# WKV7 recurrence of a two-block kernel: scores and turns on four quarters of the array, two banks for crossing products, products with v apart, state by scalar products

## The reference

```python
def wkv7_scan(s0, r, w, kk, a, k, v):
    def step(s, inp):
        r_t, w_t, kk_t, a_t, k_t, v_t = inp
        s_kk = jnp.einsum('bhvk,bhk->bhv', s, kk_t)
        s = (s * w_t[:, :, None, :] - s_kk[..., None] * (kk_t * a_t)[:, :, None, :]
             + v_t[..., None] * k_t[:, :, None, :])
        return s, jnp.einsum('bhvk,bhk->bhv', s, r_t)
    xs = tuple(jnp.moveaxis(t, 1, 0) for t in (r, w, kk, a, k, v))
    s_final, ys = lax.scan(step, s0, xs)
    return jnp.moveaxis(ys, 0, 1), s_final
```

## Time and profile before

| | |
|---|---|
| median of 3 runs | 3311.26 us (3309.19 to 3319.1) |
| the profiled execution | 3302.93 us, span 3301.3 us |
| PE busy over the span | 2858.2 us (87%) |
| DVE, ACT, POOL busy | 1932.0, 1372.7, 536.4 us |
| mean granted clock of PE | 0.942 |

### The profile page before, as it was taken

How to read it: one execution, slowest core, us unless ns; L and a number is a source line. 1 busy time by engine, 2 the same in 40 slices (tenths; PEclk the granted TensorE clock), 3 DMA queues, 4 the chain that set the end, 5 groups by cost and what they waited for, 6 DMA issues and landing times. The chain is left out here.

```text
span 3301.3 us, 70036 instructions
## 1 busy us (share of the span) xinstructions
PE 2858.2 (87%) x30245; PEld 2351.2 (71%) x30245; DVE 1932.0 (59%) x3065; ACT 1372.7 (42%) x2028; POOL 536.4 (16%) x489
## 2 busy tenths in 40 slices
PE   7998799989989569999735999999965987769999
PEld 2564678788778448887515999999963754548877
DVE  5431455666565345765663888888875146456652
ACT  2002445444444322212213777777753345333331
POOL 3001445454344110000001000000010025100000
PEclk9999899999999789999966999999987999889999
DMA  4643000000000128664306999999951210122322
GB/s 193 220 153 104 6 20 20 20 20 20 20 3 4 65 87 309 268 252 172 112 15 260 365 371 363 372 371 362 371 207 61 99 53 18 51 78 90 102 101 78
DMA packets 74015, 483.10 MB, mean 146 GB/s; under 512 B 11123, under 2 KB 13043, under 8 KB 32288
## 3 DMA queue, kind: packets, MB, share of 16 engines
q1 hardware_dynamic: 59360, 418.48, 34.0%
q0 software_dynamic: 12096, 52.43, 4.3%
q10 hardware_dynamic: 2304, 8.39, 0.6%
HBM read 457.73 MB, written 34.13 MB: 149 GB/s over the span
## 5 line engine op out<-in xcount | busy, mean ns | idle before, releaser
L2156 DVE TENSOR_TENSOR sb_moe_w_lo<-w_ring,sb_moe_w_hi 128x1408 fp32r<-128x1408 f32 (+1 forms) x132 | 255.2, 1934 | 67.7 <-ACT sb_moe_w_hi L2110 67.5
L2056 PE MATMUL ps<-sb_moe_w_hi,sb_x_feat_lo 128*128 128x352 f32 x832 | 274.3, 330 | 11.5 <-DVE sb_moe_w_lo L2156 11.5
L2058 PE MATMUL ps<-sb_moe_w_hi,sb_x_feat_hi 128*128 128x352 f32 x832 | 268.4, 323 | 0.0
L2057 PE MATMUL ps<-sb_moe_w_lo,sb_x_feat_hi 128*128 128x352 f32 x832 | 267.8, 322 | 0.0
L2110 ACT ACTIVATE sb_moe_w_hi<-w_ring 128x2816 fp32r<-128x2816 f32 x80 | 204.1, 2553 | 0.1
L2056 PEld LDWEIGHTS ps<-sb_moe_w_hi,sb_x_feat_lo 128*128 128x128 f32 x832 | 157.0, 189 | 17.3 <-issue 17.0
L2056 PE MATMUL ps<-sb_moe_w_hi,sb_hid_feat_lo 128*128 128x256 f32 x572 | 163.3, 285 | 3.9 <-DVE sb_hid_feat_lo L2182 3.9
L2058 PE MATMUL ps<-sb_moe_w_hi,sb_hid_feat_hi 128*128 128x256 f32 x572 | 161.9, 283 | 0.0
L2057 PE MATMUL ps<-sb_moe_w_lo,sb_hid_feat_hi 128*128 128x256 f32 x572 | 161.9, 283 | 0.0
L1321 DVE STREAM_TRANSPOSE sb_tb<-sb_tb 128x128 f32<-128x128 f32 x384 | 106.0, 298 | 93.6 <-ACT sb_tb L1230 91.5
L231 PE MATMUL ps<-sb_ffn_features,sb_hi_ffn 128*128 128x512 f32 x352 | 140.2, 398 | 22.1 <-DVE sb_lo_ffn L219 22.1
(11 more groups left out here) (511 smaller groups left out, 7924.3 us busy)
## 6 DMA issues: line engine op xcount, KB each, us to landing
w_ring<-w_moe_up SPq DMA_DIRECT2D x67, 1408.0 KB, 8.3
sb_hm<-w_ada SPq DMA_DIRECT2D x48, 1024.0 KB, 6.9
w_ring<-w_ffn SPq DMA_DIRECT2D x22, 1024.0 KB, 4.8
w_ring<-w_up SPq DMA_DIRECT2D x22, 1024.0 KB, 4.9
sb_t_again<-w_moe_up SPq DMA_DIRECT2D x13, 1408.0 KB, 8.5
sb_hm<-w_moe_up SPq DMA_DIRECT2D x13, 1408.0 KB, 8.3
sb_b_again<-w_moe_up SPq DMA_DIRECT2D x13, 1408.0 KB, 7.9
w_ring<-w_moe_down SPq DMA_DIRECT2D x13, 1408.0 KB, 7.6
```

The source lines that it names most:

```text
L2056: pe.matmul(out, x_lo, w_hi, start=first, stop=False)
L2057: pe.matmul(out, x_hi, w_lo, start=False, stop=False)
L2058: return pe.matmul(out, x_hi, w_hi, start=False, stop=end)
L2156: return V.tensor_tensor(WL[:, s, w], raw[raw_at(c, i)[0]][:, w], WH[:, s, w].bitcast(F32), ALU.subtract)
```

## The change

`score` and `trans` become one item. Products with FB and turns of FA and FK stay on the head's own quarter, in bank `i`; products with FK and turns of FB and v go from the head's rows to the other head's columns (`both_ways`), into one of two crossing banks, 4 + i mod 2. The order alternates: two own, two crossing. The masks are then applied in two operations (`LKE` on the own bank, `LKO` on the crossing one), and ACT copies in two (`trO`, then `trE`).

`akv` is split. `akA` stands ahead of the quad's scores, four in a row, each in its own bank. `akO` holds all that doesn't depend on the chain: K with v, v with the score matrix (latent), and the contribution of K and v to the next state. It reads the crossing tiles, goes from the other rows to the own columns, and stands behind each X of level 0. ACT copies it out, the state part in two copies of 64 columns, multiplied with the decay of the direction (`PE2`).

`Z` has 4 matmuls instead of 8 and stands ahead of `Y`, which has 8 instead of 12. The state on DVE: `ends` at U's place (old state times decay plus akO's part, both from SBUF, one operation of 64 columns for each direction), and `z` at Z's place (Z's result from PSUM times decay plus `ends`, one for each direction). Y's result is added to akO's part on DVE instead of copied by ACT. The tile AT is four wide, and every second quad uses the buffer of the receptance rows (RB) for it. A chunk has as many matmuls as before: 108 latent, 88 context.

```diff
-            for i in range(4):
-                out += [(p, f"score{n}") for n in cur[i:i + 1]]
-                out += [(pp, f"akv{n}") for n in prev[i:i + 1]]
-                out += [(p, f"trans{n}") for n in cur[i:i + 1]]
+            out += [(pp, f"akA{n}") for n in prev]
+            out += [(p, f"score{n}") for n in cur]
             out += [(p, f"first{n}") for n in cur]
             links = []
             for n in prev:
-                links += [[(pp, f"U{n}")], [(pp, f"Y{n}")] * lat(n) + [(pp, f"Z{n}")] * (n < NCH - 1)]
+                links += [[(pp, f"U{n}")], [(pp, f"Z{n}")] * (n < NCH - 1) + [(pp, f"Y{n}")] * lat(n)]
...
                         out.append((p, f"{head}{lev}.{n}"))
+                        if head == "X" and lev == 0:
+                            out.append((p, f"akO{n}"))
...
                             if n >= 4:
-                                pe.wait_ge(act_f.sem, act_f.at(f"t{LAST}.{n - 4}", p))
+                                pe.wait_ge(act_c.sem, act_c.at(f"akA{n - 4}", p))
...
+                            if i >= 2:
+                                pe.wait_ge(act_f.sem, act_f.at(f"trO{n - 2}", p))
+                                pe.wait_ge(dve_f.sem, dve_f.at(f"LKO{n - 2}", p))
...
+                            out_bank = 4 + i % 2
                             for d in range(2):
...
+                                for half in range(1 + lat(n)):
+                                    to = d * P + half * CH
+                                    for hh, oo in both_ways:
+                                        x_in = FR[hh, d, chunk_at(n, d) - CTX:chunk_at(n, d) - CTX + CH] if half else FA[hh, d, at(d)]
+                                        pe.matmul(ps[hh, i, to:to + CH], FB[hh, d, at(d)], x_in, start=True, stop=True)
+                                    for hh, oo in both_ways:
...
+                                        pe.matmul(ps[oo, out_bank, to:to + CH], FK[hh, d, at(d)], x_in, start=True, stop=True)
+                                for o, (own, other) in enumerate(((FA[:, d, at(d)], FK[:, d, at(d)]), (FB[:, d, at(d)], v[:, at(d)]))):
+                                    to = 256 + d * P + o * CH
+                                    for hh, oo in both_ways:
+                                        pe.matmul(ps[hh, i, to:to + CH], own[hh], ident[hh, hh], start=True, stop=True)
+                                    for hh, oo in both_ways:
+                                        last = pe.matmul(ps[oo, out_bank, to:to + CH], other[hh], ident[hh, hh], start=True, stop=True)
...
+                        elif head == "akO":
+                            pe.wait_ge(dve_f.sem, dve_f.at(f"LKO{n}", p))
...
+                                for hh, oo in both_ways:
+                                    last = pe.matmul(ps[hh, out_bank, to:to + CH], M[oo, 1, d, 0, :], tr[oo, 1, d, 1, :],
+                                                     start=True, stop=True)
...
                         elif head == "U":
-                            pe.wait_ge(act_c.sem, act_c.at(f"akv{n | 3}", p))
+                            pe.wait_ge(act_c.sem, act_c.at(f"akA{n}", p))
+                            if n < 8:
+                                pe.wait_ge(act_f.sem, act_f.at(f"akO{(n | 3) + 4}", p))
...
+                            S.activation(TR[:, s, i, 1].rearrange("p d o n -> p (d o n)"), ps[:, 4 + i % 2, 256:512],
+                                         ACT.Copy).then_inc(*act_f.did(f"trO{n}"))
+                            act.wait_ge(dve_f.sem, dve_f.at(f"LKE{n}", p))
+                            S.activation(TR[:, s, i, 0].rearrange("p d o n -> p (d o n)"), ps[:, i, 256:512],
+                                         ACT.Copy).then_inc(*act_f.did(f"trE{n}"))
...
+                                for d in range(2):
+                                    c = chunk_at(n, d) // CH
+                                    S.activation(ATs[s][:, i, 3, d, :], bank[:, 2, d, :], ACT.Copy, scale=PE2[:, p % 2, d, c:c + 1])
+                            S.activation(ATs[s][:, i, 1:2 + lat(n)].rearrange("p a d n -> p (a d n)"), ps[:, 4 + i % 2, 0:P * (1 + lat(n))],
+                                         ACT.Copy).then_inc(*act_f.did(x))
...
+                        elif head == "U" and 0 < n < NCH - 1:
+                            dve.wait_ge(act_f.sem, act_f.at(f"akO{n}", p))
+                            dve.wait_ge(dve_c.sem, dve_c.at(f"z{n - 1}", p))
+                            for d in range(2):
+                                c = chunk_at(n, d) // CH
+                                last = V.scalar_tensor_tensor(out=Zs[:, d, :], in0=Zb[:, n % 2, d, :], scalar=PE2[:, u, d, c:c + 1],
+                                                              in1=ATs[s][:, i, 3, d, :], op0=ALU.mult, op1=ALU.add)
```

181 lines of the change are left out of this document (100 added, 81 removed).

## The result

The changed kernel took **3330.3 us** (median of 7 runs, 3323.9 to 3334.4) against 3311.3 us of the kernel before (median of 7, 3304.5 to 3319.1). The ratio is 1.0056, with a 95% interval from 1.0043 to 1.0069: slower by a good half per cent, where 3265 had been forecast, in a range up to 3335, and faster. The profiled execution took 3329.7 us with a span of 3328.1. The 27 us between the two profiles lie in the recurrence: from the first score to the last Y it took 773 us before and 800 after.

A forecast was written before the change was run, and what follows sets the result against it. PE's queue was taken as the bound, busy 86.8 of 96 us a pair. Terms summed to -5.0 us a pair, -40 in eight, plus -6.5 in the closing quad: 3265 us, range 3245 to 3335.

The forecast's parts named there:

- Four quarters: Scores and turns on PE: own and crossing quarters run at once and need half the slots, -10.3 us a pair.
- borders: Between crossing akO products and X products on PE: last and first slots run side by side, -2.4 us a pair.
- The step that failed: Scores and turns: quarters at once need half the slots, 88 fewer; -10.3 us a pair taken, bounds 0 and -10.3.
- U behind akO: First U of each quad waits for the last akO's three ACT copies: +3.1 us a pair (2 to 5).
- The tail: Between last score and first X, PE waits for DVE's masks and `first`: 1.5 us uncovered, +3.2 us a pair.
- The crossing bank: Third score of a quad waits for the first's bank: 0.3 us a quad, +0.9 us a pair.
- akA ahead of the scores: Last akA and first score wait for ACT copies, 0.3 and 0.1 us in three quads: +1.2 us a pair.
- Work on DVE and the rest: About 5 us a pair more on DVE, mostly hidden except in the second quad's ladder: +1.2 us a pair.
- The state: State on DVE: decay product moved to U's place, so POOL's holds delay U less, -1.9 us a pair.
- The second block: Rival, chance 0.25: POOL holds both decay products on DVE in turn, +7.8 us in each of seven pairs, 3319 us.
- four quarters don't overlap: Rival, chance 0.10: own and crossing quarters on PE don't run at once, 11.8 us more a pair, 3359 us.
- DVE and ACT set the pace: Rival, chance 0.27: added DVE work lands in full in two ladders, leaving -1.4 us a pair, 3294 us.

The follow-up runs named there:

- e2: Changed kernel with every score and turn matmul issued four times over, onto the same result; executed once, 3820.7 us.
- e1: Changed kernel with all own products and turns of a chunk issued before all crossing ones, so two quarters work at a time; 3334.9 us, ratio 1.0084.
- e3: Changed kernel with another DVE order at the end of the scores: `first` operations moved ahead of or between the last masks; 3315.4 us, ratio 1.0029.
- j1: Changed kernel with the edits of both e1 and e3; 3333.3 us, ratio 1.0072.
- e6: Kernel before the change with every score and turn matmul issued four times over, at the pace of two quarters; executed once, 3792.8 us.
- k2: e3 with one full-width gate matmul of each pair moved from the third quad's ladder to the middle of its scores; 3331.1 us, ratio 1.0069.
- g1: e3 with the next pair's first exponential and its ACT table load moved behind the four akA copies; 3317.1 us, ratio 1.0013.
- e5: Changed kernel with the state computed in the old manner, by sums and a multiplication by the decay; 3350.3 us, ratio 1.0128.
- f1: Kernel before with only a new state form: ACT multiplies old state by decay, DVE does product and sum from PSUM; 3288.7 us, ratio 0.9919.
- k1: f1 with the product of old state and decay on DVE, two operations of 64 columns, instead of ACT copies; 3302.3 us, ratio 0.9976.

## Why the prediction was wrong

**Four quarters.** The step held as far as it went: eight records start in a slot, the slots fell by 11.4 us a pair and not by 12.7, 1.3 less than forecast, which the trace does not divide between scores and borders. The rule of the Trainium skill on row groups ("TensorE: Matmul & The Clock Gate", "The mechanism"), weighed there, isn't borne out here: a weight load of the crossing quarter starts at 713.22, 0.02 us behind the start of a matmul of its neighbour in the same row group (713.20), which is in flight until 713.42.

**The step that failed** is the sentence "if crossing and own quarters run at once they need half", with its bounds of 0 and -10.3. It priced a slot by the array and took for granted that PE would have the instructions; idle time for want of them stands in the sum at nothing. The runs showed in its place that the instructions for 128 matmul records come in one packet at a time, 3.7 us apart in e2's scores, while four quarters are through with 128 in 1.87 us. The idle inside the scores came at 5.4 us a pair for 0.9: the 4.5 us more are 36 us in eight pairs, the larger part of the 65 us between 3265 and 3330. Taken as a whole the term of -82 us (eight times -10.3) was worth 5 to 9 us (e1), or 14 to 18 beside e3's order on DVE (j1). e2 and e6 show the cause together with the packets of q8; e1 and k2 show that the hold-ups shrink or go when the pace does. The trace of before held nothing up, so it could not show this limit as such. It did show 34 records a us as the highest pace of small matmuls anywhere over 16 or more of them, and packets of q8 that never start less than 3.2 us apart. A bound should have been drawn from these, or at least a rival.

Two slips of the sum are small beside this. The parts given for *U behind akO* add up to 1.14 us a quad and not 1.03, +3.4 a pair and not +3.1. And the range of 3245 to 3290 is said to follow from the bounds of the terms, but the bound of 0 for the first term alone would give 3347; the prediction had put that case into a rival.

**The tail** was forecast at 1.5 us where nothing covers it and came at 1.46 to 1.49; with the wide matmuls ahead of it 2.7 a pair came for 3.2. **The crossing bank** came at 0.34 a quad for 0.3. **U behind akO** came at 2.9 for 3.1. These held.

**akA ahead of the scores** was mis-sized. I took two short waits in each quad from the latencies and didn't look at what stands in ACT's queue there: in third quads it is a table load and an exponential, 2.1 us. It came at 2.0 us a pair for 1.2, and in g1, which moves the load behind the akA copies, the wait came back inside the scores.

**Work on DVE and the rest** came at 3.5 us a pair for 1.2. Part of the difference is a wait that I didn't have, 1.7 us a pair of idle before akO. By what ended it, half (0.86 us) is ACT's copies that clear the crossing banks of the first two akO, and nearly as much (0.80) DVE's xs. Another part is the hold-ups by packets between X, T and akO products, 8.7 us over the eight pairs. Both are read from the trace of after and not tried by a run of their own.

**The state.** The forecast gain in front of U came (-2.1 for -1.9), and e5 shows the form to be worth 20 us in the changed kernel. In the kernel before it is worth 20 with the product of the old state on ACT (f1) and 5 with it on DVE (k1). The second block does happen, and I had argued it away by the two short copies. There POOL's next product started at 328.70 with no idle before it, and the second copy (328.71 to 328.89) was not held; why it was not, no run shows. In the changed kernel two short operations can be held by two POOL products in turn:

```profile
618.65 3.45 POOL L873 TENSOR_TENSOR sb_sg<-sb_a,sb_kk 128x1536 f32<-128x1536 f32 x1
...
622.02 6.94 DVE L1374 SCALAR_TENSOR_TENSOR sb_Z_sum<-sb_Z,sb_pend,sb_r_rows 128x64 f32<-128x64 f32 x2
622.06 3.43 POOL L876 TENSOR_TENSOR sb_ex<-sb_ex,sb_kk 128x1536 f32<-128x1536 f32 x1
...
625.44 3.44 POOL L880 TENSOR_TENSOR sb_sg<-sb_sg,sb_Pi 128x1536 f32<-128x1536 f32 x1
...
629.50 0.43 DVE L1385 SCALAR_TENSOR_TENSOR sb_Z<-ps,sb_pend,sb_Z_sum 128x64 f32<-128x64 f32 x2
```

The first product starts at 622.02, as one POOL product ends and 0.04 us ahead of the record of the next, and lasts until 625.57; the second lasts until 628.96: 6.94 us for two operations of 64 columns. (Sizes and means of all 160, and the wait of U in half of the quads:)

```profile
L1374 DVE SCALAR_TENSOR_TENSOR sb_Z_sum<-sb_Z,sb_pend,sb_r_rows 128x64 f32<-128x64 f32 x80 | 49.2, 655 | 0.0
...
L1374 DVE SCALAR_TENSOR_TENSOR sb_Z_sum<-sb_Z,sb_pend,sb_at 128x64 f32<-128x64 f32 x80 | 32.8, 450 | 0.0
...
L1142 PE MATMUL ps<-sb_at,sb_tb 64*64 64x64 f32 x384 | 26.2, 226 | 17.8 <-DVE sb_Z L1385 8.3 <-issue 5.6 <-ACT sb_r_rows L1281 3.9
```

Of the 80 links of the changed kernel four had both of their products of the old state held for over 1 us and eight had one; 14 more of the 160 operations took between 0.5 and 1 us. That is 1.5 links a pair with a long hold and half a link with two; only two links lasted over 5 us. The rival needed two or three doubly held links in a pair, so its condition was not met. The sum of DVE's time in these products is 88 us, where L1335 had 59 in all its 88 operations. The Trainium skill says ("SBUF — State Buffer", "Who interferes with whom") that the second to come is held for the whole of the other's operation. The rows agree that a held operation ends only as a POOL product ends. Who came first they do not show everywhere: at 622.02 DVE's record starts first and is held all the same.

**Of the rivals**, "four quarters don't overlap" fell, and its price of 94 us with it. "DVE and ACT set the pace" had the sign of the rest but not its size. 3319 of the second block came nearest, by another cause. The time stood inside the range, near its upper end, but not for a reason that the range had been drawn for, which is luck; the sign was wrong. No case had a limit that the change itself would bring up.

## What to carry to other kernels

When a change makes one resource of an engine faster (here the array's quarters), look for the highest pace at which that engine has taken instructions in the trace, and let no forecast exceed it without a reason. Small matmuls at two quarters (34 records a us) already stood at what a long burst on four gets here (32 to 36); wide ones have room. When the profile ends an idle time with "issue", set the packets of the instruction queue beside it. And take a long change apart before adopting it: of this one the new form of the state was worth 20 us (e5), and the others together cost 40.
